# Gain of queries and keys moved into the rope tables, low halves one window later, attention steps in a new order

## The chip, the cores and the metric

The kernel runs on one NeuronCore of one Trainium2 chip. The metric is the device time of one execution in microseconds (us). The engines are called as the profile calls them: PE is TensorE, DVE is VectorE, ACT is ScalarE, POOL is GpSimd, SP is SyncE, which here only issues DMAs. Each engine works through its own list in order; only semaphores tie the lists together.

## What is computed

Two transformer blocks, 256 tokens wide 1024. The first has adaLN modulation, a retention group and a differential attention group that share one input projection, an output projection and a product-key expert layer; the second a feed-forward, a gated mixer with a state-space part, another feed-forward and a gate. The change touches the attention of the first block alone, and what runs beside it:

```
def diff_softmax_attend(q, k, v, lam):
    s = jnp.einsum('bhpqd,bhpkd->bhpqk', q, k).astype(jnp.float32) * (DIFF_D ** -0.5)
    p = jax.nn.softmax(s, axis=-1)
    a = (p[:, :, 0] - lam * p[:, :, 1]).astype(v.dtype)
    return jnp.einsum('bhqk,bhke->bhqe', a, v)
...
    q = apply_rope(qk_heads(dq, qk_norm_g[0]), cos, sin)
    k = apply_rope(qk_heads(dk, qk_norm_g[1]), cos, sin)
    kc = qk_heads(cdk, qk_norm_g[1])
```

`qk_heads` cuts a row of 512 into 8 pieces of 64, divides each by its root mean square and multiplies it by a gain `g` of 64 numbers, one for queries and one for keys. `apply_rope` is `x * cos + rot(x) * sin`, where `rot` swaps neighbouring groups of 16 and changes a sign. The keys of the context (`kc`) get the gain but no rope. There are 4 heads with 2 maps each, 256 queries (2 blocks of 128) and 512 keys (256 of the context, 256 of the sequence).

## The kernel before

Weights stream from DRAM in 257 chunks of 1 MB through three buffers (`raw`). A chunk is two halves, and most halves `u` are split in two: ACT copies the high part (`w_hi`), DVE subtracts it to get the low part (`w_lo`). PE multiplies high by high, high by low and low by high, all accumulated in PSUM, so it needs both parts. There are four slots of each. SP issues a chunk when the low parts of the chunk three earlier are made.

The first stage, about the first 227 us of 1717, is the one that is changed. Its work is one list, written by hand in `front_steps`. Each engine's program walks through the same list and does its own part of each step, so the place of a step in the list sets its order on PE, DVE and ACT at once. The steps that matter:

- `win(p, h)` is a **window**: PE does one half of the input projection, pass p (0 to 5, groups of 512 columns in the order 3, 4, 5, 0, 1, 2), quarter h (0 to 3). Passes 0, 1, 2 and 4 have four token tiles and full width, pass 3 has its two context tiles at half width, pass 5 has two tiles only. On ACT and DVE a window means `ahead`: they make high and low parts up to three windows in front of PE.
- `evac p`: ACT copies the finished pass from PSUM (4 or 2 instructions).
- `mod n`: one column block of the adaLN modulation, one DVE instruction over 128x1024 and a short read of its accumulator.
- `square n`, `unit n`, `rope n`: normalisation and rope of queries (n = 0, 1), keys (2, 3) and context keys (4, 5, no rope); rope 4, 5 are the retention group's. In `unit`, DVE sums the squares, multiplies the 512 columns by the gain, waits for ACT's square root and inverts it; for keys it also multiplies by the result.
- `qturn h`, `kturn h`: PE transposes (2 or 4 of 128x128), ACT copies the result. `kturn 0` waits for `s_qk` 6, which is the end of unit 5.
- `score n` (n = 0 to 7: block n // 4, head n % 4): PE two score matmuls of 512 columns; DVE the `combine` of n - 1 (1 / sum, factor, `aa = E1 * c + E0`, L1992), then two maxima (L2199); ACT two exponentials. `turn n`: PE transposes `aa` (L1069), ACT copies it to `aT`. `weigh n`: PE `aT` by the values. After `weigh 3` and `weigh 7` ACT also scales and squares four heads.
- `rturn`, `mask`, `madd`, `rscore`, `rweigh`, `dnorm`, `dblocks`: the retention group's transposes, decay masks, scores and sums, and the turned attention result. `out n` is the output projection; PE's first `out` ends the stage.

Score n + 1, weigh n - 1 and turn n stand together between windows, with the window in front of them as cover for the combination. At three places no window stands there: score 2, weigh 0, turn 1; score 4, weigh 2, turn 3; weigh 6, turn 7, rturn 0. Lines of helpers: L911 is every matmul, L992 the transposes of `head_turn`, L1069 those of `turn`, L1511 every ACT instruction, L1980 DVE's tensor_tensor, L2000 its sums, L2004 its reciprocals, L2136 `mod`. `ar` is the arena that holds nearly all intermediate tiles, `cols` and `rows` are small tables, `pb` is PSUM.

Of the kernel before, what the change touches and what calls it, by code (L numbers as in the profile page):

```python
# [12 lines left out]
ACT = mybir.ActivationFunctionType  # L13
# [149 lines left out]
def front_steps():  # L163


    steps = []

    def mods(*ns):
        steps.extend(("mod", n) for n in ns)

    def win(p, h, *more):
        steps.append(("win", p, h))
        steps.extend(more)

# [12 lines left out]
    steps.extend([("whalf", 3), ("cturn", 2), ("crows", 2)])  # L187
    win(0, 3, ("evac", 0))
# [8 lines left out]
    win(2, 0, ("square", 2), ("square", 3), ("unit", 2), ("qturn", 0), ("qturn", 1))  # L197
    mods(22)
    win(2, 1, ("rope", 2), ("unit", 3), ("qturn", 2), ("qturn", 3))
    mods(23)  # L200
    win(2, 2, ("rope", 3), ("square", 4), ("square", 5))
    mods(24)
    win(2, 3, ("evac", 2), ("unit", 4))
    win(3, 0, ("unit", 5))
    mods(25, 26)
    win(3, 1, ("kturn", 0), ("kturn", 1))
    mods(27)
    win(3, 2, ("kturn", 2), ("kturn", 3), ("score", 0))
    mods(28)
    win(3, 3, ("evac", 3), ("score", 1), ("turn", 0))  # L210
    mods(29)
    steps.extend([("score", 2), ("weigh", 0), ("turn", 1)])
    win(4, 0, ("score", 3), ("weigh", 1), ("turn", 2))
    mods(30, 31)
    steps.extend([("score", 4), ("weigh", 2), ("turn", 3)])
    win(4, 1, ("score", 5), ("weigh", 3), ("turn", 4), ("rope", 4))
    mods(32, 33)
    win(4, 2, ("score", 6), ("weigh", 4), ("turn", 5), ("rope", 5))
    mods(34, 35)
    win(4, 3, ("evac", 4), ("score", 7), ("weigh", 5), ("turn", 6))  # L220
    mods(36, 37)
    mods(38, 39)
    steps.extend([("weigh", 6), ("turn", 7), ("rturn", 0)])
    win(5, 0, ("mask", 0), ("weigh", 7))
    win(5, 1, ("rturn", 1), ("mask", 1), ("madd", 0))
    win(5, 2, ("rscore", 0), ("mask", 2), ("dvar", 0), ("madd", 1))
    win(5, 3, ("added", 1), ("droot", 0), ("rscore", 1), ("evac", 5), ("madd", 2), ("dnorm", 0))
# [170 lines left out]
def program(nc, wall, keys_d, cols_d, rows_d, bigrows_d, crow_d, wmod_d, dist_d, x_d, ctx_d, pT_d, gws_d, out_d, n_chunks):  # L398
    assert n_chunks * 2 == U_END
    with ExitStack() as es:  # L400
# [380 lines left out]
        def heads8(ap):  # L781
            return ap.rearrange("p (h d) -> p h d", d=64)
# [124 lines left out]
        def tensor_program(e):  # L907
# [109 lines left out]
            for name, n, *more in FRONT:  # L1017
# [24 lines left out]
                elif name == "kturn":  # L1042
                    t.wait_ge(s_qk, 6)
                    if n >= 2:
                        t.wait_ge(s_heads, 4 + n - 1)
                    head_turn(5 + n % 2 * 2, [pj(i, 2048 + n * 128, 2176 + n * 128) for i in range(4)])
                elif name == "rturn":
# [8 lines left out]
                elif name == "score":  # L1056
                    i, h = n // 4, n % 4
                    for p in range(2):
                        t.wait_ge(s_heads, 8)
                        if n:  # L1060
# [440 lines left out]
        def scalar_program(e):  # L1501
            a = Engine(e, s_a)
            made = 0
# [122 lines left out]
            for name, n, *more in FRONT:  # L1626
# [346 lines left out]
        def vector_program(e):  # L1973
# [31 lines left out]

            def ahead(u, only=False):
# [145 lines left out]
            def unit(n, ap):  # L2152
# [4 lines left out]
                ts(r_, r_, 1.0 / 64, EPS, MUL, ADD, sig=s_qn)  # L2157
                g_ = qkg[:, 0:64] if n < 2 else qkg[:, 64:128]
                tt(heads8(ap), heads8(ap), bc(g_, 1, 8), MUL)
                v.wait_ge(s_qs, n + 1)  # L2160
# [48 lines left out]
            for name, n, *more in FRONT:  # L2209
# [32 lines left out]
                elif name == "win" and (n, *more) != (5, 3):  # L2242
                    ahead(HALF_OF[(name, n, *more)])
                elif name == "unit":
                    v.wait_ge(s_wev, group_done(3 if n < 2 else 4))
                    unit(n, pj(n, 1536, 2048) if n < 2 else pj(n - 2, 2048, 2560))
                elif name == "rope":
                    if n < 2:
                        rope(pj(n, 1536, 2048), n, s_qk)
                    elif n < 4:  # L2250
                        rope(pj(n - 2, 2048, 2560), n - 2, s_qk)
                    else:
                        v.wait_ge(s_wev, group_done(0))
                        rope(pj(n - 4, 0, 512), n - 4, s_rk)
                elif name == "added":
# [635 lines left out]
```

## Time and profile before

| | |
|---|---|
| median of 3 runs | 1717.91 us (1717.3 to 1718.87) |
| profiled execution, its own time | 1718.86 us |
| its span in the trace | 1717.1 us |
| PE / DVE / ACT busy, share of the span | 96% / 74% / 56% |
| HBM | 184 GB/s over the span |
| first stage, to PE's first `out` matmul | 226.45 us |

The profiled execution is 0.95 us above the median, which is inside the spread of the runs, so differences read from the trace may be taken off the median as they stand. Times in the rows below count from the start of the span.

### The profile page before, as it was taken

To read this page: it belongs to the slowest core of one execution; us is meant where nothing else is said; L and a number is where in the kernel's file an instruction comes from. 1 tells how busy PE (TensorE), PEld (TensorE's weight loads), DVE (VectorE), ACT (ScalarE), POOL (GpSimd) and SP (SyncE) were. 2 spreads that over 40 slices of the span, in tenths; PEclk is the share of its full clock that TensorE was granted. 3 is DMA by queue.
4 is the path that set the end of the run, shared out by engine and by line. 5 is a ranking of instruction groups with operands and counts; after the bars stand their busy time and mean duration, and the time that the engine had idled before them with its cause. 6 is when DMAs were issued, how large, how long until landed. Compare 5 with 4: busy or idle time off the path is not lost.

```text
span 1717.1 us, 26934 instructions
## 1 busy us (share of the span) xinstructions
PE 1640.3 (96%) x10312; PEld 1398.2 (81%) x10312; DVE 1276.1 (74%) x2066; ACT 968.9 (56%) x1343; POOL 73.3 (4%) x46
## 2 busy tenths in 40 slices
PE   8988788998999999999999999999998989999997
PEld 3776578998999888888888888788888778788886
DVE  2686666899888899987777766776666787676666
ACT  4555455554455554555555555665556767665556
POOL 0000003532000000000000000000000000000000
PEclk9999898999999999999999999999999999999999
DMA  8643334445655555566656565455544533554552
GB/s 319 248 177 120 100 131 148 148 164 193 195 187 188 179 194 213 191 220 252 219 208 214 193 226 185 166 193 199 191 177 160 196 135 135 184 215 172 196 192 78
DMA packets 53267, 317.86 MB, mean 185 GB/s; under 512 B 5937, under 2 KB 6097, under 8 KB 19218
## 3 DMA queue, kind: packets, MB, share of 16 engines
q1 hardware_dynamic: 51954, 310.08, 51.0%
q0 software_dynamic: 1184, 6.05, 0.9%
q8 instruction: 82, 1.34, 0.3%
q14 instruction: 47, 0.39, 0.1%
HBM read 306.64 MB, written 9.47 MB: 184 GB/s over the span
## 4 chain that ended last, share of the span: by engine, by line
PE 75%; DVE 17%; ACT 5%; issue 1%; DMA 1%; DVEq 0%; ACTq 0%; SPq 0%
PE pb L911 74%; DVE w_lo L1980 4%; DVE ar L1980 4%; ACT ar L1511 2%; DVE ar L1992 2%; ACT w_hi L1511 1%; DVE ar L2136 1%; DVE ar L2342 1%; DVE ar L2339 1%; DMA raw<-in_wall 1%; ACT L1511 1%; DVE ar L2346 1%; DVE sm L2199 0%; DVE ar L1985 0%; ACT HX L1511 0%
## 5 line engine op out<-in xcount | busy, mean ns | idle before, releaser
L1980 DVE TENSOR_TENSOR w_lo<-raw,w_hi 128x1024 fp32r<-128x1024 f32 x471 | 577.3, 1226 | 198.1 <-ACT w_hi L1511 166.6
L1511 ACT ACTIVATE w_hi<-raw 128x1024 fp32r<-128x1024 f32 x498 | 528.7, 1062 | 144.2 <-PE pb L911 103.2
L911 PE MATMUL pb<-HX,w_hi 128*128 128x256 f32 (+1 forms) x2752 | 509.0, 332 | 7.6 <-DVE HX L1980 3.5
L911 PEld LDWEIGHTS pb<-HX,w_hi 128*128 128x128 f32 x2752 | 413.8, 192 | 51.0 <-issue 4.0
L911 PE MATMUL pb<-w_hi,HC 128*128 128x512 f32 (+1 forms) x1648 | 443.9, 391 | 4.4 <-DVE HC L1992 3.3
L911 PEld LDWEIGHTS pb<-w_hi,HC 128*128 128x128 f32 x1648 | 302.3, 188 | 65.2 <-issue 3.8
L1511 ACT ACTIVATE ar<-pb 128x256 f32<-128x256 f32 (+2 forms) x320 | 153.4, 480 | 327.1 <-PE pb L911 221.1
L1980 DVE TENSOR_TENSOR ar<-ar 128x512 bf16<-128x512 bf16 (+7 forms) x494 | 263.3, 568 | 44.9 <-ACT ar L1511 21.3
L911 PE MATMUL pb<-HX,w_lo 128*128 128x256 f32 x1952 | 279.3, 284 | 2.5 <-DVE w_lo L1980 2.2
L911 PEld LDWEIGHTS pb<-HX,w_lo 128*128 128x128 f32 x1952 | 263.9, 192 | 14.5 <-DVE w_lo L1980 3.3
L911 PE MATMUL pb<-w_lo,HC 128*128 128x512 f32 (+1 forms) x824 | 252.9, 388 | 0.0
L911 PEld LDWEIGHTS pb<-w_lo,HC 128*128 128x128 f32 x824 | 154.6, 188 | 32.5
L911 PE MATMUL pb<-w_hi,HX 128*128 128x512 f32 x512 | 145.0, 406 | 3.5 <-ACT w_hi L1511 2.0
L911 PE MATMUL pb<-ar 128*128 128x64 bf16 (+3 forms) x1960 | 125.6, 222 | 19.3 <-ACT ar L1511 9.2
L911 PEld LDWEIGHTS pb<-ar 128*128 128x128 bf16 (+2 forms) x1960 | 104.6, 119 | 42.2 <-issue 19.8
L911 PEld LDWEIGHTS pb<-w_hi,HX 128*128 128x128 f32 x512 | 95.9, 194 | 25.3 <-ACT w_hi L1511 4.3
L1511 ACT ACTIVATE ar<-ar 128x512 f32<-128x512 f32 (+8 forms) x112 | 66.9, 597 | 75.8 <-DVE ar L1980 31.5
L1511 ACT ACTIVATE HC<-ar 128x512 fp32r<-128x512 f32 (+1 forms) x89 | 55.4, 623 | 83.0 <-PE pb L911 46.9
L1980 DVE TENSOR_TENSOR ar<-pb,ar 128x512 f32<-128x512 f32 (+1 forms) x86 | 58.4, 680 | 52.2 <-ACT ar L1511 44.2
L1980 DVE TENSOR_TENSOR HC<-ar,HC 128x512 fp32r<-128x512 f32 (+1 forms) x89 | 60.6, 681 | 32.4 <-ACT HC L1511 27.7
L911 PE MATMUL pb<-w_lo,HX 128*128 128x512 f32 x256 | 81.4, 400 | 0.5 <-DVE w_lo L1980 0.3
L2738 POOL TENSOR_TENSOR w_lo<-raw,w_hi 128x1024 fp32r<-128x1024 f32 x27 | 64.9, 2404 | 104.3 <-ACT w_hi L1511 63.6
(146 smaller groups left out, 688.9 us busy)
## 6 DMA issues: line engine op xcount, KB each, us to landing
raw<-in_wall SPq DMA_DIRECT2D x257, 1024.0 KB, 4.8
ar<-in_wmod SPq DMA_DIRECT2D x24, 512.0 KB, 3.8
act_keep<-ar SPq DMA_DIRECT2D x28, 256.0 KB, 5.6
ar<-act_keep SPq DMA_DIRECT2D x28, 256.0 KB, 5.0
x<-in_wmod SPq DMA_DIRECT2D x8, 512.0 KB, 5.2
ar<-in_bigrows POOLq DMA_DIRECT2D x2, 1024.0 KB, 5.0
ar<-acs_keep POOLq DMA_DIRECT2D x2, 1024.0 KB, 8.8
x<-in_x SPq DMA_DIRECT2D x1, 1024.0 KB, 9.6
```

The lines of the kernel that those rows point to most:

```text
L911: return e.matmul(o, l, r, start=start, stop=stop, skip_group_check=True)
L1511: a.did(e.activation(out, in_, func, scale=scale, **kw), sig)
L1980: v.did(e.tensor_tensor(out, a_, b_, op), sig)
L1992: v.did(e.scalar_tensor_tensor(out, a_, s_, b_, op0, op1), sig)
L2136: v.did(e.scalar_tensor_tensor(w, w, 1.0, c_, MUL, MUL, accum_out=modT[:, n, 0:1]), s_modv)
L2339: v.did(e.max(vals[:, c_], src))
L2342: v.did(e.max_index(idx[:, c_], vals[:, c_], src))
L2346: v.did(e.match_replace(src, vals[:, c_], src, NEG))
L2738: p.did(e.tensor_tensor(w_lo[:, made % NH, :], raw_half(w), w_hi[:, made % NH, :].bitcast(F32), SUB), s_lop)
```

## The change

- **Gain.** `unit` no longer multiplies by the gain. A new step `ropetab`, once, multiplies the cosine and sine tables by the gains of queries and keys (six small DVE instructions, into unused columns of `yv`). Rope 0 to 3 use these tables. The context keys, which have no rope, get the gain when ACT copies the turned keys: that copy of 512 columns becomes two of 256, the second with a scale per partition (`kg`, one new column of `cols`). The tensors behind `cols` keep their addresses.
- **Rope** writes its swapped half in two DVE instructions of 256 columns, where there were four of 128.
- **Low parts.** On DVE `ahead` reaches two windows in front of PE from pass 1 on (three before). The high parts stay three in front.
- **Banks and waits.** `kturn` uses PSUM banks 7 and 6 (5 and 7 before), so it doesn't share a bank with the scores, and a score waits for its own head's keys alone; `turn` waits for all.
- **Order.** `qturn` stands in front of the squares and units of its window. Squares 4, 5 and units 4, 5 stand behind window (2, 3), evac 2. The key turns stand one window earlier, the scores, turns and weighings are spread so that a window stands in front of each, up to (5, 2). `mod` steps move to fit, and with them the places of their DMAs, which are worked out from the list.

```
-                tt(heads8(ap), heads8(ap), bc(g_, 1, 8), MUL)
...
+            def rope_tables():
+                v.wait_ge(s_tab, 32)
+                for z in range(2):
+                    g_ = qkg[:, 64 * z:64 * z + 64]
+                    tt(scaled_cos[z].rearrange("p (t d) -> p t d", t=2), col("cos").rearrange("p (t d) -> p t d", t=2),
+                       bc(g_, 1, 2), MUL, free=True)
...
+                    for b in range(2):
+                        tt(so[:, :, :, b, :], si[:, :, :, b, :], bc(ga[:, :, 1 - b, :], 1, 2), MUL, free=True)
...
-                    for a_ in range(2):
-                        tt(tv[:, :, a_, b, :], xv[:, :, a_, 1 - b, :], bc(sv[:, a_, b, :], 1, 8), MUL, free=True)
+                    tt(tv[:, :, :, b, :], xv[:, :, :, 1 - b, :], bc(sv[:, :, b, :], 1, 8), MUL, free=True)
...
-                while made < (ORD[u] + 1 if only else REACH[u]):
+                while made < (ORD[u] + 1 if only else REACH[u] - late):
...
-                    ahead(HALF_OF[(name, n, *more)])
+                    ahead(HALF_OF[(name, n, *more)], late=int(n >= 1))
...
-                    act(kTd[:, n, :], PB[5 + n % 2 * 2][:, :], ACT.Copy, sig=s_heads)
+                    act(kTd[:, n, 0:256], PB[7 - n % 2][:, 0:256], ACT.Copy)
+                    act(kTd[:, n, 256:512], PB[7 - n % 2][:, 256:512], ACT.Copy, scale=col("kg"), sig=s_heads, free=True)
...
-                        t.wait_ge(s_heads, 8)
+                        t.wait_ge(s_heads, 4 + h + 1)
...
-    win(2, 3, ("evac", 2), ("unit", 4))
-    win(3, 0, ("unit", 5))
+    win(2, 3, ("evac", 2), ("square", 4), ("square", 5), ("unit", 4), ("unit", 5))
```

**DVE, from window (0, 3) to rope 0.** Before; the two `w_lo` are those of windows (0, 3) and (1, 0), the instruction on `ar<-ar,rows` is the gain, L2136 is mod 18:

```order
30 L1980 TENSOR_TENSOR w_lo<-raw,w_hi 128x1024
31 L2136 SCALAR_TENSOR_TENSOR ar,modT<-ar 128x1024
32 L1980 TENSOR_TENSOR w_lo<-raw,w_hi 128x1024
33 L1980 TENSOR_TENSOR HC<-fsc,HC 128x256 x2
34 L2000 TENSOR_REDUCE ar<-ar 128x8
35 L1987 TENSOR_SCALAR ar<-ar 128x8
36 L1980 TENSOR_TENSOR ar<-ar,rows 128x512
37 L2004 RECIPROCAL ar<-ar 128x8
```

Now, on the same engine and the same stretch (lines are three further on):

```order
30 L1983 TENSOR_TENSOR w_lo<-raw,w_hi 128x1024
31 L1983 TENSOR_TENSOR ar<-cols,rows 128x128
32 L1983 TENSOR_TENSOR ar<-cols,rows 128x4x16 x2
33 L1983 TENSOR_TENSOR ar<-cols,rows 128x128
34 L1983 TENSOR_TENSOR ar<-cols,rows 128x4x16 x2
35 L2139 SCALAR_TENSOR_TENSOR ar,modT<-ar 128x1024
36 L1983 TENSOR_TENSOR HC<-fsc,HC 128x256 x2
37 L2003 TENSOR_REDUCE ar<-ar 128x8
38 L1990 TENSOR_SCALAR ar<-ar 128x8
39 L2007 RECIPROCAL ar<-ar 128x8
```

The low part of window (1, 0) has moved behind the first unit, the six table instructions stand in its place, and the reciprocal follows the short scalar step directly.

**PE, from window (4, 3) to window (5, 1).** Before; 128x512 on `ar` are score matmuls, 128x128 on `ar` are weighings, L1069 are turns, L992 is rturn:

```order
181 L911 MATMUL pb<-w_hi,HC 128x512 x4
182 L911 MATMUL pb<-w_lo,HC 128x512 x2
183 L911 MATMUL pb<-ar 128x512 x2
184 L911 MATMUL pb<-ar 128x128 x4
185 L1069 MATMUL pb<-cols,ar 128x128 x4
186 L911 MATMUL pb<-ar 128x128 x4
187 L1069 MATMUL pb<-cols,ar 128x128 x4
188 L992 MATMUL pb<-cols,ar 128x128 x6
189 L911 MATMUL pb<-w_hi,HX 128x512 x4
190 L911 MATMUL pb<-w_lo,HX 128x512 x2
```

Now, from the second tile of window (5, 0) on; score 6, weigh 4 and turn 5 stand three rows before it:

```order
185 L912 MATMUL pb<-w_hi,HX 128x512 x4
186 L912 MATMUL pb<-w_lo,HX 128x512 x2
187 L912 MATMUL pb<-ar 128x512 x2
188 L912 MATMUL pb<-ar 128x128 x4
189 L1071 MATMUL pb<-cols,ar 128x128 x4
190 L912 MATMUL pb<-w_hi,HX 128x512 x4
191 L912 MATMUL pb<-w_lo,HX 128x512 x2
192 L912 MATMUL pb<-w_hi,HX 128x512 x4
193 L912 MATMUL pb<-w_lo,HX 128x512 x2
194 L912 MATMUL pb<-ar 128x128 x4
195 L1071 MATMUL pb<-cols,ar 128x128 x4
196 L993 MATMUL pb<-cols,ar 128x128 x6
```

Before, score 7, weigh 5, turn 6, weigh 6, turn 7 and rturn 0 stood in one piece. Now window (5, 0) ends before score 7, weigh 5, turn 6, and window (5, 1), two tiles, stands before weigh 6, turn 7, rturn 0.

## Rows read from the trace of the kernel before

**Rows 1.** The page, part 1: busy us (share of the span) xinstructions.
```profile
PE 1640.3 (96%) x10312; PEld 1398.2 (81%) x10312; DVE 1276.1 (74%) x2066; ACT 968.9 (56%) x1343; POOL 73.3 (4%) x46
```

**Rows 2.** Windows: stretch, length, busy of each engine, PEclk, DMA share, GB/s.
```profile
60.00:93.00 33.00, 33.00 (x153) 27.26 (x152) 24.82 (x60) 19.55 (x31) 0.00 (x0) 1.00 0.51 185
93.00:120.60 27.60, 23.22 (x113) 18.76 (x111) 25.26 (x46) 14.43 (x23) 0.00 (x0) 1.00 0.41 152
120.60:211.70 91.10, 76.81 (x356) 57.47 (x356) 58.01 (x108) 46.78 (x96) 0.00 (x0) 0.91 0.35 122
```

**Rows 3.** Waits in 93:227 us, one each of PE, DVE: us, times, longest.
```profile
PE pb L1069 <- DVE ar L1992: 6.9, 3, 3.3
...
DVE w_lo L1980 <- ACT w_hi L1511: 22.4, 7, 5.7
```

**Rows 4.** Timeline of DVE: start, duration, line, instruction [idle before <-releaser].
```profile
69.20 0.43 DVE L1980 TENSOR_TENSOR HC<-fsc,HC 128x256 fp32r<-128x256 f32 x1 [1.82 <-ACT HC L1511]
...
96.76 0.69 DVE L1980 TENSOR_TENSOR ar<-ar,rows 128x512 f32<-128x512 f32 x1
97.56 0.20 DVE L2004 RECIPROCAL ar<-ar 128x8 f32<-128x8 f32 x1
...
98.59 1.23 DVE L2136 SCALAR_TENSOR_TENSOR ar<-ar 128x1024 f32<-128x1024 f32 x1
...
99.93 1.23 DVE L1980 TENSOR_TENSOR w_lo<-raw,w_hi 128x1024 fp32r<-128x1024 f32 x1
101.19 1.50 DVE L1980 TENSOR_TENSOR ar<-ar,cols 128x512 f32<-128x512 f32 x5
102.72 0.69 DVE L1980 TENSOR_TENSOR ar<-ar 128x512 f32<-128x512 f32 x1
```

**Rows 5.** Timeline of ACT: square root of unit 2, one exponential of score 5.
```profile
96.76 0.21 ACT L1511 ACTIVATE ar<-ar 128x8 f32<-128x8 f32 x1 [0.53 <-DVE ar L1987]
...
166.61 0.78 ACT L1511 ACTIVATE ar<-pb,sm,ar 128x512 f32<-128x512 f32 x1 [4.11 <-DVE sm L1980]
```

**Rows 6.** Timeline of PE: key turns, a whole iteration, and the stage's last steps.
```profile
120.66 1.55 PE L992 MATMUL pb<-cols,ar 128*128 128x128 f32 x8 [1.99 <-DVE ar L1980]
121.87 2.05 PE L911 MATMUL pb<-w_hi,HX 128*128 128x512 f32 x4
...
157.64 1.18 PE L911 MATMUL pb<-w_hi,HX 128*128 128x512 f32 x4
...
163.29 2.22 PE L911 MATMUL pb<-ar 64*128 64x512 f32 x12
165.34 0.60 PE L1069 MATMUL pb<-cols,ar 128*128 128x128 f32 x4
165.70 1.17 PE L911 MATMUL pb<-w_hi,HX 128*128 128x512 f32 x4
...
206.75 1.99 PE L911 MATMUL pb<-ar 64*128 64x256 f32 x8 [1.05 <-ACT ar L1511]
...
211.07 0.61 PE L911 MATMUL pb<-w_lo,HX 128*128 128x512 f32 x2
...
226.45 1.61 PE L911 MATMUL pb<-w_hi,HC 128*128 128x512 f32 x4 [2.49 <-DVE HC L1992]
```

**Rows 7.** Timeline of DVE: combination 4, maxima 5, and the stage's end.
```profile
163.86 0.16 DVE L2004 RECIPROCAL sm<-ar 128x1 f32<-128x1 f32 x1
...
165.05 1.28 DVE L2199 TENSOR_REDUCE sm<-pb 128x1 f32<-128x512 f32 x2
166.37 0.16 DVE L1980 TENSOR_TENSOR sm<-sm,ar 128x2 f32<-128x2 f32 x1
...
212.58 1.50 DVE L1992 SCALAR_TENSOR_TENSOR ar<-pb,ar 128x512 f32<-128x512 f32 x2
...
225.48 1.65 DVE L1992 SCALAR_TENSOR_TENSOR HC<-pb,cols,HC 128x256 fp32r<-128x256 f32 x4
```

**Rows 8.** The page, part 6, weight chunks: count, KB each, us to landing.
```profile
raw<-in_wall SPq DMA_DIRECT2D x257, 1024.0 KB, 4.8
```

More of the change, by code:

```diff
@@ L196, in front_steps @@
     mods(21)
-    win(2, 0, ("square", 2), ("square", 3), ("unit", 2), ("qturn", 0), ("qturn", 1))
+    win(2, 0, ("qturn", 0), ("qturn", 1), ("square", 2), ("square", 3), ("unit", 2))
     mods(22)
-    win(2, 1, ("rope", 2), ("unit", 3), ("qturn", 2), ("qturn", 3))
+    win(2, 1, ("qturn", 2), ("qturn", 3), ("rope", 2), ("unit", 3))
     mods(23)
-    win(2, 2, ("rope", 3), ("square", 4), ("square", 5))
+    win(2, 2, ("rope", 3))
+    win(2, 3, ("evac", 2), ("square", 4), ("square", 5), ("unit", 4), ("unit", 5))
@@ L202, in front_steps @@
     mods(24)
-    win(2, 3, ("evac", 2), ("unit", 4))
-    win(3, 0, ("unit", 5))
[L205 to L212, printed above, removed]
-    win(4, 0, ("score", 3), ("weigh", 1), ("turn", 2))
-    mods(30, 31)
-    steps.extend([("score", 4), ("weigh", 2), ("turn", 3)])
-    win(4, 1, ("score", 5), ("weigh", 3), ("turn", 4), ("rope", 4))
@@ L217, in front_steps @@
-    mods(32, 33)
-    win(4, 2, ("score", 6), ("weigh", 4), ("turn", 5), ("rope", 5))
+    win(3, 0, ("kturn", 0), ("kturn", 1))
+    mods(25)
+    win(3, 1, ("kturn", 2), ("kturn", 3), ("score", 0))
+    mods(26)
+    win(3, 2, ("score", 1), ("turn", 0))
+    mods(27, 28)
+    win(3, 3, ("evac", 3), ("score", 2), ("weigh", 0), ("turn", 1))
+    mods(29, 30)
+    win(4, 0, ("score", 3), ("weigh", 1), ("turn", 2))
+    mods(31, 32)
+    win(4, 1, ("score", 4), ("weigh", 2), ("turn", 3), ("rope", 4))
@@ L219, in front_steps @@
+    mods(33)
+    win(4, 2, ("score", 5), ("weigh", 3), ("turn", 4), ("rope", 5))
     mods(34, 35)
-    win(4, 3, ("evac", 4), ("score", 7), ("weigh", 5), ("turn", 6))
+    win(4, 3, ("evac", 4), ("score", 6), ("weigh", 4), ("turn", 5))
     mods(36, 37)
[L222 to L226, printed above, removed]
@@ L227, in front_steps @@
-    win(5, 3, ("added", 1), ("droot", 0), ("rscore", 1), ("evac", 5), ("madd", 2), ("dnorm", 0))
+    win(5, 0, ("score", 7), ("weigh", 5), ("turn", 6))
+    mods(38)
+    win(5, 1, ("weigh", 6), ("turn", 7), ("rturn", 0), ("mask", 0))
+    mods(39)
+    win(5, 2, ("weigh", 7), ("rturn", 1), ("mask", 1), ("madd", 0))
+    win(5, 3, ("rscore", 0), ("mask", 2), ("dvar", 0), ("madd", 1), ("added", 1), ("droot", 0), ("rscore", 1), ("evac", 5),
+        ("madd", 2), ("dnorm", 0))
     steps.extend([("rweigh", 0), ("rscore", 2), ("mask", 3), ("rweigh", 1), ("dblocks", 0), ("madd", 3)])
@@ L616, in program @@
         s1, s2 = yv[:, 0, 0:512], yv[:, 1, 0:512]
+        scaled_cos = [yv[:, 0, 512 + 256 * z:640 + 256 * z] for z in range(2)]
+        scaled_sin = [yv[:, 0, 640 + 256 * z:768 + 256 * z] for z in range(2)]
         mrow = [yv[0:2, b, 512:1024] for b in range(2)]
@@ L1043, in tensor_program @@
                     t.wait_ge(s_qk, 6)
-                    if n >= 2:
+                    if n:
                         t.wait_ge(s_heads, 4 + n - 1)
-                    head_turn(5 + n % 2 * 2, [pj(i, 2048 + n * 128, 2176 + n * 128) for i in range(4)])
+                    head_turn(7 - n % 2, [pj(i, 2048 + n * 128, 2176 + n * 128) for i in range(4)])
                 elif name == "rturn":
@@ L2004, in rcp, with ahead @@
                 v.did(e.reciprocal(out, a_), sig)
-            def ahead(u, only=False):
+            def ahead(u, only=False, late=0):
                 nonlocal made
-                while made < (ORD[u] + 1 if only else REACH[u]):
+                while made < (ORD[u] + 1 if only else REACH[u] - late):
                     w = SPLIT[made]
@@ L2246, in vector_program @@
                     unit(n, pj(n, 1536, 2048) if n < 2 else pj(n - 2, 2048, 2560))
+                elif name == "ropetab":
+                    rope_tables()
                 elif name == "rope":
                     if n < 2:
-                        rope(pj(n, 1536, 2048), n, s_qk)
+                        rope(pj(n, 1536, 2048), n, s_qk, scaled_cos[0], scaled_sin[0])
                     elif n < 4:
-                        rope(pj(n - 2, 2048, 2560), n - 2, s_qk)
+                        rope(pj(n - 2, 2048, 2560), n - 2, s_qk, scaled_cos[1], scaled_sin[1])
                     else:
                         v.wait_ge(s_wev, group_done(0))
-                        rope(pj(n - 4, 0, 512), n - 4, s_rk)
+                        rope(pj(n - 4, 0, 512), n - 4, s_rk, col("cos"), col("sin"))
                 elif name == "added":
```

16 lines of the change are left out of this document (9 added, 7 removed).

## The prediction, made before the changed kernel was run

> **What bounds the kernel now.** I read the busy shares first. PE is busy 96% of the span and DVE 74% [rows 1], so a saving on DVE counts only where PE stands still for it. The table of windows says where that is: PE is busy all of 60 to 93 us, then 23.2 of 27.6 us, then 76.8 of 91.1 us [rows 2]. In the second of these stretches DVE is busy 25.3 of 27.6 us and bounds; in the third no engine is near full, and the granted clock of PE is 0.91. A mean of 0.91 is a mix of its two levels, 2.4 GHz and 1.2 GHz, with 18% of the time (16.4 us) at the lower one. The waits name two links: turns of `aa` wait 6.9 us for the combinations, and DVE waits 22.4 us for high parts that ACT makes in the same step [rows 3]. The timeline then gives the three dates on which I hang the sum: key turn 0 at 120.66, end of window (5, 3) at 211.7, first `out` at 226.45 [rows 6]. Behind `out` nothing is changed, so what `out` gains the end gains, as long as weights arrive.
>
> **Part 1, to key turn 0 (DVE bounds).** Removed in front of it: six gain products, 0.80 us each from start to next start [rows 4]. But the reciprocal behind each now meets ACT's square root, which it did not before: the root starts with the product at 96.76 and takes 0.21 [rows 5], so with two handoffs about 0.3 of each 0.8 comes back; 6 x 0.5 = 3.0 us. Rope: the first five instructions take 101.19 to 102.72 [rows 4]; one of 512 columns needs about 0.73, so the four of 128 take 0.20 each. The trace has no such instruction of 256 columns. It lies between 0.20 (no cost for length) and 0.40 (no fixed cost); on the line through the sizes shown it is 0.35 to 0.38. Then two of them cost 0.7 to 0.75 where four cost 0.8: 0.1 for each of four ropes, 0.4 us, with bounds 0 and 1.6. One low part fewer (99.93 to 101.19, 1.3) and one mod fewer (98.59 to 99.93, 1.3) stand in front of unit 5. The softplus exchange with ACT in `gammas` doesn't follow fully, since ACT comes to it out of a PSUM copy bound by PE: 0.3 us back. The tables are six instructions, four of them at 0.20 and two of about 0.3, 1.4 us with bounds 1.2 and 2.2. They stand where DVE idled 1.82 us before the context's low parts [rows 4], and the low part of window (1, 0), 1.3 us, has left the same place, so 3.1 us cover them: nothing. If that cover were gone they would cost 1.4. Sum: 3.0 + 0.4 + 1.3 + 1.3 - 0.3 = 5.7, key turn 0 at 115.0. PE gets there earlier still: it came at 118.7 (120.66 less 1.99), window (3, 1), 4.2 us as worked out below, now stands behind the turn, and of the 4.4 us that PE idled in stretch two [rows 2] the 2.4 that were not this wait were for the query turns' copy, which now stands in front of the squares, and for a PSUM copy. So PE comes at 112.1 and waits 2.9 us instead of 1.99. I expect the clock to fall as it fell after that 1.99: the next four matmuls took 2.05 against 1.18 at full clock [rows 6]. For turns and window together 1.8 us.
>
> **Part 2, to the end of window (5, 3).** PE's own work: 76.8 busy, less half of the 16.4 us at the lower clock, is 68.6 us at full clock [rows 2]. Window (3, 1) comes in: a full window takes 157.64 to 163.29, 5.65 for four tiles, so two full and two half tiles 4.2. Retention score 0 leaves, 2.0 [rows 6]. So 70.8 us, and with the clock's 1.8 PE alone could end at 115.0 + 72.6 = 187.6. Do the chains keep up? PE's iteration is 157.64 to 165.70, 8.06 us: window 5.65, score and weighing 2.05, turn 0.36 [rows 6]. From the end of a score: maxima 1.5, exponentials 2 x 0.9 [rows 5, 7], combination 1.2 (163.86 to 165.05), 4.5 us in all, and a turn comes 1.0 + 0.4 + 5.65 + 2.05 = 9.1 after that score. DVE also does two mods (2.7) and a low part (1.3): 6.7 us, with a rope 8.9. The low part's high part was made one window ago, so the DVE-on-ACT waits of rows 3 go. I walked the list with these numbers: score 0 at 122.9 (129.4 before), turn 0 at 129.4 after 0.3 of waiting for the combination, turn 1 at 136.1, turn 2 at 144.1, turn 3 at 152.2, turn 4 at 160.3, turn 5 at 168.3, each without a wait. In pass 5 a window has two tiles, 2.85 us, and no longer covers DVE's 6.7: turn 6 waits 1.2 and comes at 174.7, weigh 6 waits 0.8 for ACT's copy, turn 7 0.4 and comes at 180.0. Windows (5, 2) and (5, 3), weigh 7 and rturn 1 end at 188.3 (before 211.7). The split copies of turned keys, 0.2 us more on ACT each, lie beside windows: nothing. Low parts are there 7 us before PE wants them, except at (3, 0), where DVE is done at 107.1 and PE asks at 108.4.
>
> **Part 3, to `out`.** Retention score 0 waits for ACT's copy of rturn 1, to 188.8. Before, DVE's products of score 0 started at 212.58 and the low parts that release `out` at 225.48 [rows 7], 12.9 us. Now mask 2 is in that chain as before, the products start 1.0 after their score, the second has to wait 0.3 for its half, and one low part more (the one put off) stands in it, 1.3: 12.9 + 1.3 + 0.3 = 14.5, then 1.0 to `out`. 188.8 + 1.0 + 14.5 + 1.0 = 205.3, a gain of 21.2 us. The walk leaves out handoffs on some ten links, 0.06 to 0.1 us each, 0.8 us. **Gain 20.4 us**.
>
> **Queues.** SP issues a chunk when low parts are made, so one window (5.65 us) later. A chunk lands in 4.8 us [rows 8] and its high part is made some four windows after the issue: covered, and 5 us at worst if not. Mod DMAs move with the list; mod 36, the tightest, is issued when mod 32 is done, about 147, and used about 170. POOL's only part here is the gate row after weigh 7; it follows.
>
> **Rivals.** (a) **The clock stays low**: gaps of 2.9 us at the key turn and 0.4 to 1.2 us around pass 5 leave PE at 1.2 GHz over pass 5 too. Each stretch costs about 2 us, as the key turn's; two to four of them, 4 to 7 us: gain 13 to 17. For it: 18% of stretch three was at the low level. Against: PE's waits there shrink from 14.3 us to about 3. The Trainium skill (TensorE: Matmul & The Clock Gate, HAM oscillation) says that short runs of matmuls between waits bring the clock down every time; the drops of rows 2 agree, and by it they should go with the gaps. (b) **Only the DVE savings count**: the chain score, exponential, combination is longer than I take it, for each window ends on it as turns did before. Then key turn 0's 5.7 us stays, and of the turns' 6.9 us of waiting [rows 3] some part up to the whole: gain 6 to 12, time 1706 to 1712. (c) **Nothing moves**: PE is 96% busy, and what the stage gives is taken back behind it, where weights or the expert layer set the pace: 1717.9. The Trainium skill (Perfetto Trace Analysis, Identifying the Most-Contended Engine) says to work on the engine with the highest occupancy first; by that DVE edits give 0. Rows 2 speak against it, with 18.7 us of PE idle in two stretches, and that page's Optimization Strategy allows for a bottleneck that changes with the regime. (d) **Slower: low parts come last.** With the reach cut to two, if DVE is over one window behind PE from (3, 0) on, PE waits in each of the 12 windows to (5, 3) for one mod and one low part, 2.6 us: 31 us, against 20 gained, 1728. It decides once DVE's slack falls from 7 us under 0. Against: DVE's 6.7 to 8.9 us a window against 8.06.
>
> **How the numbers follow.** Forecast case, gain 18 to 24: 0.70. (a) 0.14, (b) 0.09, (c) 0.03, (d) 0.04. The profiled execution's sum goes off the median as it stands: 1717.9 - 20.4 = 1697.5. The forecast case reaches 1694 to 1700; the bounds of rope and tables add 1.2 below and 2 above; with (a) to 1705 that holds 0.84. Range 1693 to 1705.5. A measurement tells about 0.2% (3.4 us) from no change. Faster 0.93, same 0.03, slower 0.04.
>
> **What would show it.** Right: no DVE wait on `w_hi` between 120 and 190; key turn 0 at 115 with 2.9 us of PE idle before it; turns 1 to 5 some 8.1 us apart without waits; first `out` at 206. Wrong: turns 1 to 5 each after a wait (b), granted clock under 0.9 in 170 to 190 (a), PE waiting for `w_lo` (d), or `out` at 206 and an end that is not 20 us earlier (c).

## The result, and the profile after

The changed kernel takes 1699.1 us (median of 4 runs, 1697.9 to 1702.5), against 1718.2 for the kernel before on the same chip: a ratio of 0.9892, with a 95% interval of 0.9875 to 0.9910, or 19.1 us. Run again word for word on two later occasions it took 1699.2 both times. The prediction was 1697.5, in a range of 1693 to 1705.5. The profiled execution has a span of 1697.4 us and took 1699.2.

The busy shares of the page (compare [rows 1]) hardly differ: DVE lost 4.4 us of 1276, PE 8.5 of 1640.

```profile
PE 1631.8 (96%) x10312; PEld 1394.2 (82%) x10312; DVE 1271.7 (75%) x2054; ACT 969.6 (57%) x1347; POOL 72.7 (4%) x46
```

Its span is 19.7 us shorter (1717.1 to 1697.4). 11.2 of that is idle time of PE that is gone; the other 8.5 is PE's busy time, for the same 10312 matmuls, and it goes with the higher granted clock of the stretch that follows the key turns. The table of windows (columns as in [rows 2]), cut at key turn 0, at retention score 0 and behind the first `out`:

```profile
60.00:93.00 33.00, 33.00 (x153) 27.30 (x152) 24.17 (x61) 20.56 (x32) 0.00 (x0) 1.00 0.45 157
93.00:115.00 22.00, 18.41 (x90) 15.56 (x89) 18.88 (x35) 11.53 (x20) 0.00 (x0) 0.94 0.45 167
115.00:190.00 75.00, 71.85 (x368) 54.83 (x367) 59.93 (x104) 46.60 (x99) 0.00 (x0) 0.97 0.45 155
190.00:208.00 18.00, 12.64 (x70) 9.99 (x69) 14.31 (x25) 13.55 (x21) 1.22 (x2) 0.90 0.25 84
208.00:1697.00 1489.00, 1445.95 (x9456) 1264.90 (x9454) 1133.23 (x1788) 848.73 (x1136) 71.16 (x39) 0.99 0.52 185
```

From 115 to 190 PE is busy 71.85 of 75 us, at a granted clock of 0.97; before, the like stretch had 76.8 of 91.1 at 0.91 [rows 2]. The last line answers to the rest of the program: 1489 us before too, with 1445.6 us of PE.

All waits of PE in 93 to 210 us (total, times, longest), which answer to [rows 3]; none is for a low part or for weights:

```profile
PE pb L993 <- DVE ar L1983: 3.6, 1, 3.6
PE pb L912 <- DVE HC L1995: 2.7, 1, 2.7
PE pb L927 <- DVE ar L1983: 1.9, 1, 1.9
PE pb L912 <- ACT ar L1513: 1.5, 2, 1.0
PE pb L1071 <- DVE ar L1995: 1.5, 2, 1.2
PE pb L912 <- DVE ar L1995: 0.8, 1, 0.8
```

And this is all that DVE waited for between 120 and 190 us; the wait on `w_hi`, 22.4 us in 93 to 227 us before, is not among it:

```profile
DVE sm L2212 <- PE pb L912: 6.3, 4, 4.5
```

The timeline of DVE (compare [rows 4]): the tables, the idle time behind them, a unit without its gain product, the one unit (2) that waits longer for its square root, and a rope:

```profile
63.27 1.03 DVE L1983 TENSOR_TENSOR ar<-cols,rows 128x128 f32<-128x128 f32 x6
...
67.85 0.43 DVE L1983 TENSOR_TENSOR HC<-fsc,HC 128x256 fp32r<-128x256 f32 x1 [2.22 <-ACT HC L1513]
...
109.93 0.17 DVE L1990 TENSOR_SCALAR ar<-ar 128x8 f32<-128x8 f32 x1
110.38 0.20 DVE L2007 RECIPROCAL ar<-ar 128x8 f32<-128x8 f32 x1 [0.28 <-ACT ar L1513]
...
95.06 0.20 DVE L2007 RECIPROCAL ar<-ar 128x8 f32<-128x8 f32 x1 [0.71 <-ACT ar L1513]
...
72.82 2.09 DVE L1983 TENSOR_TENSOR ar<-ar 128x512 f32<-128x512 f32 x4
```

The same rope, read from a view that is cut at 74 us and so ends with its third instruction:

```profile
72.82 1.36 DVE L1983 TENSOR_TENSOR ar<-ar 128x512 f32<-128x512 f32 x3
```

The timeline of PE (compare [rows 6]): key turn 0 and what follows it, key turns 2 and 3, some turns of `aa`, retention score 0, the first `out`:

```profile
113.56 1.97 PE L993 MATMUL pb<-cols,ar 128*128 128x128 f32 x8 [3.58 <-DVE ar L1983]
115.18 2.05 PE L912 MATMUL pb<-w_hi,HX 128*128 128x512 f32 x4
...
121.23 1.03 PE L993 MATMUL pb<-cols,ar 128*128 128x128 f32 x8
...
143.77 0.60 PE L1071 MATMUL pb<-cols,ar 128*128 128x128 f32 x4
151.83 0.60 PE L1071 MATMUL pb<-cols,ar 128*128 128x128 f32 x4
159.89 0.60 PE L1071 MATMUL pb<-cols,ar 128*128 128x128 f32 x4
...
174.87 0.66 PE L1071 MATMUL pb<-cols,ar 128*128 128x128 f32 x4 [1.18 <-DVE ar L1995]
...
180.31 0.66 PE L1071 MATMUL pb<-cols,ar 128*128 128x128 f32 x4 [0.33 <-DVE ar L1995]
...
189.68 5.88 PE L912 MATMUL pb<-ar 64*128 64x256 f32 x32 [0.98 <-ACT ar L1513]
...
206.10 2.05 PE L912 MATMUL pb<-w_hi,HC 128*128 128x512 f32 x4 [2.67 <-DVE HC L1995]
```

Turns 2, 3 and 4 are 8.06 us apart and wait for nothing. The granted clock was 0.50 over key turn 0 (113.56 to 115.50 us) and 1.00 in 170 to 190 us, where the last turns stand:

```profile
113.56:115.50 1.94, 1.94 (x9) 1.94 (x10) 1.78 (x3) 0.82 (x3) 0.00 (x0) 0.50 0.00 0
170.00:190.00 20.00, 16.96 (x92) 13.07 (x91) 15.09 (x26) 14.63 (x34) 0.00 (x0) 1.00 0.22 83
```

The stage's end on DVE, with the products of retention score 0, the last two low parts, and the low parts that release `out` (compare [rows 7]):

```profile
190.84 0.69 DVE L1995 SCALAR_TENSOR_TENSOR ar<-pb,ar 128x512 f32<-128x512 f32 x1 [4.12 <-PE pb L912]
...
197.18 2.55 DVE L1983 TENSOR_TENSOR w_lo<-raw,w_hi 128x1024 fp32r<-128x1024 f32 x2
...
205.13 1.65 DVE L1995 SCALAR_TENSOR_TENSOR HC<-pb,cols,HC 128x256 fp32r<-128x256 f32 x4
```

**A common origin.** The start of a program, before anything that the change touches, differs by up to 2.1 us between executions. Its last common step is DVE's low part of window (0, 3): at 63.48 us before, at 62.13 after, and between 62.03 and 64.14 in all profiles. So dates of different kernels are compared below as the time since that step. From it to the first `out` ("the stage") before took 162.97 us and the changed kernel 143.97: 19.0 us, all but 0.1 of the gain. From `out` to the end it is 1490.7 and 1491.3.

### The profile page after: what moved, and what is told of

It reads as the page before. It is cut to its first block, busy times and chain, and to the rows that moved or that the text cites. A ratio compares the mean times of both kernels' runs of the same rounds, so it can differ in the third digit from the quotient of the medians.

```text
span 1697.4 us, 26926 instructions
## 1 busy us (share of the span) xinstructions
PE 1631.8 (96%) x10312; PEld 1394.2 (82%) x10312; DVE 1271.7 (75%) x2054; ACT 969.6 (57%) x1347; POOL 72.7 (4%) x46
## 4 chain that ended last, share of the span: by engine, by line
PE 77%; DVE 16%; ACT 4%; DMA 1%; issue 1%; DVEq 0%; SPq 0%; ACTq 0%
PE pb L912 76%; DVE w_lo L1983 4%; DVE ar L1983 4%; DVE ar L1995 2%; ACT ar L1513 2%; DMA raw<-in_wall 1%; ACT w_hi L1513 1%; DVE ar L2357 1%; DVE ar L2354 1%; ACT L1513 1%; DVE ar L2139 1%; DVE ar L2361 1%; DVE ar L1999 0%; DVE sm L2212 0%; ACT HX L1513 0%
## 5 line engine op out<-in xcount | busy, mean ns | idle before, releaser
L1983 DVE TENSOR_TENSOR ar<-ar 128x512 bf16<-128x512 bf16 (+9 forms) x506 | 268.5, 566 | 44.6 <-ACT ar L1513 21.0
L912 PEld LDWEIGHTS pb<-HX,w_lo 128*128 128x128 f32 x1952 | 264.4, 192 | 14.5 <-DVE w_lo L1983 3.3
```

The lines of the kernel that those rows point to most:

```text
L912: return e.matmul(o, l, r, start=start, stop=stop, skip_group_check=True)
L1983: v.did(e.tensor_tensor(out, a_, b_, op), sig)
```

## The experiments

Three names for the parts of the change: the fold (gain in the tables, ropes of two parts), the late low parts, and the order. Theory: the three parts take away three different waits of one chain between DVE and PE, so each has its own price and they nearly add: the fold and the order bring key turn 0, the late low parts take DVE's waiting for ACT out of the turns. Rivals: only the DVE work saved counts, or late low parts are a risk and no gain. All experiments are copies of one of the two kernels with the edit that is shown.

### The fold alone

The kernel before, in its order and with its early low parts, gets the tables, the units without gain products, ropes of two parts and the split copy of turned keys.

```diff
-                g_ = qkg[:, 0:64] if n < 2 else qkg[:, 64:128]
-                tt(heads8(ap), heads8(ap), bc(g_, 1, 8), MUL)
...
-                    for a_ in range(2):
-                        tt(tv[:, :, a_, b, :], xv[:, :, a_, 1 - b, :], bc(sv[:, a_, b, :], 1, 8), MUL, free=True)
+                    tt(tv[:, :, :, b, :], xv[:, :, :, 1 - b, :], bc(sv[:, :, b, :], 1, 8), MUL, free=True)
```

> The order, banks and reach of before, with the gain folded into the rope tables and rope in two instructions. Theory (PE gains what it stood still for): key turn 0 comes when PE arrives, at most 2.0 us earlier plus the 1.8 us of low clock behind that wait, and about 1 us at the query turns: 1718.2 - 4 = 1714, between 1713 and 1716. Rival (the DVE work itself is what counts, 3.4 us before the key turn and 0.2 after): the same 3.5 us, but then key turn 0 would still wait. Rival (most-occupied engine alone counts): 1718.

Measured: 1714.5 us, ratio 0.9977 (0.9967 to 0.9987), 3.7 us off. PE, at key turn 0:

```profile
117.16 1.09 PE L994 MATMUL pb<-cols,ar 128*128 128x128 f32 x8 [0.25 <-DVE ar L1983]
```

It came 53.74 us after the common step, against 57.18 before: 3.44 us, for which the prediction had 3.0 + 0.4. The wait of 1.99 us is 0.25, and PE is at full clock. DVE is still the last to come: the turn moved by all that DVE saved, and PE came 1.7 us earlier too. The turns of `aa` wait as before (6.8 us against 6.9), so this part has nothing to do with them.

### The late low parts alone

```diff
-                while made < (ORD[u] + 1 if only else REACH[u]):
+                while made < (ORD[u] + 1 if only else REACH[u] - late):
...
-                    ahead(HALF_OF[(name, n, *more)])
+                    ahead(HALF_OF[(name, n, *more)], late=int(n >= 1))
```

> Before, with DVE's low parts two windows ahead of PE in place of three, nothing else. Theory: the 22 us that DVE waits for high parts of the same step go; combinations of scores 0 to 7 come up to 1.3 us plus that wait earlier, key turn 0 1.3 us earlier, and one low part more stands before out: a gain of 3 to 7 us, 1711 to 1715. Rival (d), low parts come last: PE waits for low parts from window (3, 0) on and the kernel is slower than 1718. Rival (reach is only a cover, and the turns wait for the exponentials): within 1 us of 1718.

Measured: 1711.7 us, ratio 0.9958 (0.9941 to 0.9974), 6.5 us off. The waits of DVE and PE in 93 to 227 us:

```profile
DVE w_lo L1980 <- ACT w_hi L1511: 5.0, 3, 3.4
...
PE pb L1069 <- DVE ar L1992: 3.1, 3, 2.1
```

22.4 us of DVE waiting for ACT became 5.0, and 6.9 us of PE waiting for combinations became 3.1 [rows 3]. Key turn 0 did not move (57.14 against 57.18): the one low part fewer ahead of it stood where DVE idles anyway, and that idle time only grew (from 1.82 to 3.13 us). Rival (d), in which low parts come last, is refuted: no wait of PE for `w_lo` shows in 93 to 227 us here, nor in the changed kernel. Part of the stage's 6.0 us is the clock's, though: this execution kept the full clock at key turn 0 after 1.94 us of waiting, where the profile before had not after 1.99, and from key turn 0 to key turn 2 it took 5.12 us against 6.73. That is 1.6 us which the edit did not buy.

### The changed kernel with one part undone

Early low parts in the changed kernel:

```diff
-                    ahead(HALF_OF[(name, n, *more)], late=int(n >= 1))
+                    ahead(HALF_OF[(name, n, *more)], late=0)
```

> The changed kernel with the reach of before (low parts three windows ahead). Theory: low parts wait for high parts again (over 10 us of DVE waits on w_hi between key turn 0 and window (5, 3)), the combinations behind them come later, turns 0 and 6 wait about 2 us each, key turn 0 is 1.3 us later; against that one low part leaves the end of the stage: 1699 + 1 to 4, 1700 to 1703. Rival (the order alone is the gain): 1699 or under.

Measured: 1706.8 us, ratio 0.9938 (0.9922 to 0.9955): 7.7 us lost against the changed kernel, more than I had expected. DVE waits 13.0 us for `w_hi` again, and five turns wait, 8.1 us in all. The stage took 147.49 us, 3.5 more than 143.97; but this execution kept the full clock at key turn 0, after the same idle time, and the turn came 51.41 us after the common step, not 1.3 later as I had expected:

```profile
114.83 1.09 PE L993 MATMUL pb<-cols,ar 128*128 128x128 f32 x8 [3.59 <-DVE ar L1983]
```

The gain products and ropes of four parts in the changed kernel (the first edit above undone, with the tables and the split copy left out again):

> The changed kernel with gain products in the units and four-part ropes of before, no tables. Theory: key turn 0 is 3.4 us later (six times 0.5 and four times 0.1) and nothing behind it catches up, as PE bounds from there: 1699.1 + 3.4 = 1702.5, and PE's wait before the key turn grows from 3.6 to about 7. Rival (PE's gap only shifts and the clock is low anyway): under 1701.

Measured: 1705.7 us, ratio 0.9927 (0.9910 to 0.9943), 6.6 us lost, again more than expected.

```profile
116.89 1.97 PE L993 MATMUL pb<-cols,ar 128*128 128x128 f32 x8 [5.93 <-DVE ar L1982]
```

Key turn 0 came 54.86 us after the common step against 51.43: 3.43 us, which shows as 5.93 us of waiting in place of 3.58. That it is the price of the old order (3.44) is chance: DVE idles 0.48 us ahead of the last reciprocal here, once, for a reason that the profile doesn't show. Without that the fold is worth some 3.0 us in the new order, as the kernel with the order alone, below, confirms (54.47 against 51.41 for order and fold). The stage is 3.8 us longer. So of the 6.6 us, 2.8 are not in this stage of this execution; 2.0 of them lie behind the first `out` (1493.3 us to the end, against 1491.3).

### The order alone

The changed kernel with both of these undone: its order of steps, PSUM banks and turns are what is left of the change.

> The changed kernel's order, PSUM banks and turns, with the gain products and the four-part ropes of before and the low parts where they stood before: neither the fold nor the late low parts. From the low part of window (0,3) to the first out before takes 163.0 us and the changed kernel 144.0; the fold alone took 4.1 off and the late low parts alone 6.0. If the parts add, this kernel takes 163.0 - (19.0 - 4.1 - 6.0) = 154.1 us there, and its time is about 1709 us. If the parts overlap (each alone relieves the same VectorE chain, and the order makes its own use of it), it is nearer to the two runs with one part undone: 144.0 + 3.5 + 3.8 = 151.3 us, 1706 us.

Measured: 1709.8 us, ratio 0.9941 (0.9927 to 0.9954), 9.5 us off; the stage took 153.2 us. As they stand, both are nearer the additive case (154.1, 1709) than the overlapping one (151.3, 1706). The stages don't decide it, though: they hold the clock's drops at key turn 0, of which this execution and the changed kernel's had one and the two singles none. With the drops taken out, as in the last table below, the additive case is 148.1, the overlapping one 151.2, and this kernel 150.4. Key turn 0 came 2.71 us earlier than before, at 54.47: one mod and one low part fewer in front of it, 2.6 us in the prediction. PE's waits in 93 to 227 us, and below them one of the kernel before:

```profile
PE pb L1071 <- DVE ar L1994: 8.0, 5, 2.5
PE pb L993 <- DVE ar L1982: 5.7, 1, 5.7
...
PE pb L912 <- ACT ar L1513: 1.6, 2, 1.0
```

```profile
PE pb L911 <- ACT ar L1511: 8.1, 6, 2.7
```

The order by itself makes PE come to key turn 0 far too early, and its turns of `aa` wait no less than before (8.0 against 6.9). What it takes away is another wait, which neither the prediction's list of links nor the theory above names: matmuls of PE (scores, weighings, retention scores) that wait for ACT, 8.1 us before, 7.4 with the fold alone, 7.7 with the late low parts alone, 1.6 here and 1.5 in the changed kernel. Turn 7 comes 0.8 us earlier than before (128.75 against 129.58), and by then PE has also done windows (5, 0) and (5, 1), which stood behind it; from there to `out` it is 24.5 us against 33.4. Which single move of the order brings how much of the 9.5 us was not tried.

### The price of the clock

In the changed kernel 28 useless transposes (3.2 us) go into the gap ahead of key turn 0:

```diff
                 elif name == "kturn":
+                    if n == 0:
+                        t.wait_ge(s_qk, 4)
+                        for j in range(28):
+                            e.transpose(PB[7][:, (j % 2) * 128:(j % 2) * 128 + 128], pj(j % 2, 2048, 2176), ident)
                     t.wait_ge(s_qk, 6)
```

> The changed kernel, with 28 useless transposes (about 3.4 us) in TensorE's queue in the 3.6 us gap ahead of key turn 0; they go to the bank that the turn overwrites, and need rows that were ready long before. Nothing else is changed, so the turn still waits for VectorE's last key rope. It tells the price of the wait from the price of the low clock behind it. My theory: the turn comes when it came (51.4 us after the last low part of window (0, 3)), but at the full clock: 1.09 us instead of 1.97, the window behind it 4.2 us instead of about 6.6, and all that follows 1 to 2.5 us earlier (the two profiles of the changed kernel have turns 2 and 3 at 59.1 and 58.1 us after that low part): 56.5 us there, and the time 1696.5 to 1698.5 against 1699.2. Rival: VectorE's chain to score 0 and the combinations bounds what follows, so an earlier window changes nothing: first out at 142.9 to 144.0 us and 1699.

Beside it, and once before, the changed kernel word for word:

> The changed kernel itself, word for word, beside e9_key_gap_filled on the same chip: 1697 to 1701 us, key turn 0 after 3.6 us of idle time at the low clock (1.97 us) as in the two profiles so far.

> The changed kernel itself, word for word, on the chip of the others: 1697 to 1702 us. It shows whether the key turn at the head of the last window falls to the low clock again after its wait (1.97 us for eight transposes in the first profile; an otherwise similar wait of 3.6 us left it at the full clock in another kernel), and how far the times of one kernel spread.

PE in the three, the filled one first, each with the turn and (in the two copies) the matmuls behind it:

```profile
111.80 3.22 PE L1047 MATMUL pb<-cols,ar 128*128 128x128 f32 x28
115.54 1.09 PE L993 MATMUL pb<-cols,ar 128*128 128x128 f32 x8 [0.53 <-DVE ar L1987]
```

```profile
114.90 1.97 PE L993 MATMUL pb<-cols,ar 128*128 128x128 f32 x8 [3.59 <-DVE ar L1983]
116.52 1.77 PE L912 MATMUL pb<-w_hi,HX 128*128 128x512 f32 x4
```

```profile
115.02 1.97 PE L993 MATMUL pb<-cols,ar 128*128 128x128 f32 x8 [3.58 <-DVE ar L1983]
116.64 1.90 PE L912 MATMUL pb<-w_hi,HX 128*128 128x512 f32 x4
```

Filled, the turn came when it always came (51.40 us after the common step), and all behind it came earlier. From key turn 0 to key turns 2 and 3 the filled kernel took 5.10 us, the copies 6.50 and 6.64, the first profile of the changed kernel 7.67. These 1.4 to 2.6 us are all that the low clock cost there, and they reach the first `out`: the stage took 141.49 us filled, 142.84 and 142.93 in the copies, 143.97 in the first profile. Less what the clock cost, the three are at 141.4 to 141.5 too. The times, 1698.3 us filled and 1699.2 beside it, differ by 1.0 with intervals that overlap (ratios 0.9863 to 0.9896 and 0.9871 to 0.9904): the trace shows it, the medians agree and don't prove it. The rival, that DVE bounds what follows, falls by the stage, in this one trace.

### A better place for two mods, and for two low parts

```diff
-    mods(22)
...
-    mods(23)
...
-    mods(24)
+    mods(22, 23)
     win(3, 0, ("kturn", 0), ("kturn", 1))
-    mods(25)
+    mods(24, 25)
```

> The changed kernel, with VectorE's modulation of blocks 22 and 23 (two steps of 1.3 us) put behind the key unit of the last self half instead of ahead of it. My theory: the key turn at the head of the last window waits for VectorE's chain (3.6 us idle in the changed kernel), so it comes 2.7 us earlier and TensorE's idle time there falls to about 0.9 us; scores, turns and the first out follow 2 to 3 us earlier, since VectorE has idle time between there and score 0. Time 1694 to 1697 us (changed kernel: 1699.1). Rival: the modulation that now stands later delays VectorE's next low parts or the query unit, the wait moves to a later turn, and the time stays 1698 to 1700.

Measured: 1696.9 us, ratio 0.9872 (0.9857 to 0.9886), against 1699.2 (0.9873 to 0.9902) for the changed kernel beside it: 2.3 us, with intervals that just overlap.

```profile
111.70 1.09 PE L991 MATMUL pb<-cols,ar 128*128 128x128 f32 x8 [1.54 <-DVE ar L1981]
...
125.08 0.66 PE L1069 MATMUL pb<-cols,ar 128*128 128x128 f32 x4 [0.74 <-DVE ar L1993]
...
202.43 2.04 PE L910 MATMUL pb<-w_hi,HC 128*128 128x512 f32 x4 [2.78 <-DVE HC L1993]
```

Key turn 0 came at 49.39, 2.0 us earlier where 2.7 were expected (DVE now idles 0.73 us for ACT ahead of unit 4), and at full clock. Both theories were partly right: turn 0 now waits 0.74 us for DVE, which has the moved mods in front of it, and so comes 1.4 us earlier than in the filled kernel and not 2.0. The stage took 140.12 us, 2.8 less than the changed kernel's beside it; 1.5 of that is the clock's drop that did not come.

Then, on top of it, the last two low parts behind `dblocks`, where DVE has nothing urgent:

```diff
-                    if n == 1:
-                        ahead(HALF_OF["win", 5, 3])
                 elif name == "dvar":
...
                 elif name == "dblocks":
                     turn(TB_DIFF, 4)
+                    ahead(HALF_OF["win", 5, 3])
```

> The kernel of e5_mods_behind_keys, and VectorE's last two low parts (2.55 us, between score 1 and dblocks) put behind dblocks. My theory: the tail from score 0 to the first out is bound by VectorE's chain, so out comes another 1.5 to 2.6 us earlier: 1692 to 1695 us. Rival: ScalarE's chain (evacuations and the gate's turn) ends at the same point and out comes at most 0.5 us earlier, or the low parts are then awaited by the products behind out: the same time as e5.

Measured: 1693.7 us, ratio 0.9850 (0.9835 to 0.9864), 5.5 us better than the changed kernel beside it, with intervals that are apart. PE and DVE around `out`:

```profile
202.68 1.16 PE L910 MATMUL pb<-w_hi,HC 128*128 128x512 f32 x4 [1.18 <-DVE HC L1993]
...
203.81 2.56 DVE L1981 TENSOR_TENSOR w_lo<-raw,w_hi 128x1024 fp32r<-128x1024 f32 x2
```

`out` came 138.80 us after the common step, 1.3 earlier (1.5 to 2.6 expected), with half the wait, and at full clock: four such matmuls take 1.16 us against 2.04. Retention score 3, which stands behind the first `out`, came at 141.72 against 145.51, 3.8 us earlier; the two medians differ by 3.2. So the low clock behind the 2.78 us wait had cost 2.5 us, more than the 1.3 by which `out` came earlier. This is the best of the versions run.

## Why the prediction was right, and where it was off

Dates since the common step. The prediction's are its own less 63.48, without the 0.8 us that it set aside for handoffs at the end, and are called the walk below, since it walked the list of steps; "filled" is the kernel without the clock's drop at key turn 0.

| | key turn 0 | turn 0 | turn 4 | turn 5 | turn 6 | turn 7 | score 0 | `out` |
|---|---|---|---|---|---|---|---|---|
| predicted | 51.5 | 65.9 | 96.8 | 104.8 | 111.2 | 116.5 | 125.3 | 141.8 |
| changed, first profile | 51.43 | 66.74 | 97.76 | 105.93 | 112.74 | 118.18 | 127.55 | 143.97 |
| changed, beside the filled | 51.42 | 65.57 | 96.63 | 104.80 | 111.61 | 117.05 | 126.42 | 142.84 |
| filled | 51.40 | 64.14 | 95.19 | 103.37 | 110.17 | 115.62 | 124.99 | 141.49 |

- **Part 1, 5.7 us: measured 5.75.** The order gave 2.71 (one mod and one low part, 2.6) and the fold on top of it 3.04 (3.0 + 0.4 - 0.3 = 3.1). The late low part gives nothing here: 57.14 against 57.18. The reciprocal does meet the root, with 0.28 us of waiting in five of six units. From the short scalar step to the reciprocal it is 1.00 us before and 0.44 now, so a gain product was worth 0.56 and not 0.80 (I had 0.5). In unit 2 the reciprocal waits 0.71: in the new order ACT's copy of the query turn, 0.86 us, stands ahead of that root. The prediction did not have this, and it is the 0.4 us by which the two singles (3.44 + 2.71 = 6.15) exceed the whole. The softplus exchange took back 0.45 (DVE waits 0.73 there, 0.28 before), where the prediction had 0.3; the ropes gave 0.13 each and not 0.1. That the sum is right to 0.1 is in part luck: what unit 2 lost, the other products had more than I gave them. A part of 256 columns costs some 0.33 us, where I had 0.35 to 0.38: one instruction of 512 and two of 256 take 1.36, and one of 512 alone 0.69. The tables cost nothing, as said: 1.03 us (I had 1.4), and DVE still idled 2.22 us behind them.
- **PE's wait at key turn 0, 2.9 us: measured 3.6.** PE came 0.8 us earlier than I had it. That wait is DVE's date less PE's, so it changed nothing but the odds on the clock.
- **The clock, 1.8 us: measured 2.6, 1.5 and 1.4.** This term differs from execution to execution. In the profile beside the filled kernel, in which it was 1.4, turns 0 to 5 stand within 0.4 us of the walk; in the first, in which it was 2.6, all are 0.8 to 1.1 late. Rival (a) took the clock for low over pass 5; its sign was a clock under 0.9 in 170 to 190, and it was 1.00 there. Where it did fall is a place that no term has: behind the 2.67 us wait at the first `out`, whose four matmuls take 2.05 us where they took 1.61 before. From there to retention score 3 it is 5.28 us against 4.51, and 2.92 at full clock.
- **Part 2: turns 1 to 5 without waits, as walked, 8.06 us apart (8.17 from turn 4 to 5).** The prediction counted only PE's waits for the combinations; the fall of its waits for ACT, from 8.1 us to 1.5, is in its result all the same, since it took PE's own work as the bound. Turn 6 waits 1.18 (1.2), weigh 6 0.56 (0.8), turn 7 0.33 (0.4). What is off is small: 0.4 us more on the way from turn 5 to turn 6, and 0.98 us instead of 0.5 for ACT's copy of the last turn ahead of score 0. Together 0.9 us, about the 0.8 that I had set aside for handoffs. In the first profile `out` is 2.2 us later than the walk: those 0.8, 0.8 of the clock, and 0.6 that is left.
- **Part 3, 16.5 us from score 0 to `out`: measured 16.42.** DVE's chain was 14.3 (14.5).
- **Behind `out` nothing changed, rival (c):** 1490.7 us before, 1491.3 after, 1487.5 to 1493.3 in all profiles. So `out`, 20.35 us earlier from the span's start, is 19.0 earlier by the common step, and the rest is an earlier start of that execution. That it stands at 206.10, to a tenth where the sum had it (205.3 + 0.8), is luck: 1.35 us of early start cover what the stage fell short. The gain was 1.3 us too high, 20.4 against 19.1. The prediction worked out from the Trainium skill (Perfetto Trace Analysis, Identifying the Most-Contended Engine) that DVE edits give 0. They did not: PE is at 96%, and DVE edits alone gave 3.7 and 6.5 us, since the 4% that PE idles stand in part where DVE's chain is last. The Trainium skill goes on (Perfetto Trace Analysis, Optimization Strategy) to look for the gaps on that engine and for what blocks it there; that agrees with these runs.
- **Rival (b)** falls: turns waited 6.9 us before and 1.5 after. Neither the order alone (8.0) nor order and fold (8.1) brings that; the late low parts do.

How the parts add, as stages since the common step, the clock's cost at key turn 0 taken out of each (its time from key turn 0 to 2, less 5.1; only there, so it is rough for the kernels of the old order):

| | stage | less the clock | median less before, same chip |
|---|---|---|---|
| before | 162.97 | 161.3 | 0 |
| fold alone | 158.88 | 158.9 | -3.7 |
| late low parts alone | 157.01 | 157.0 | -6.5 |
| order alone | 153.20 | 150.4 | -9.5 |
| order and fold | 147.49 | 147.5 | -11.4 |
| order and late low parts | 147.79 | 145.1 | -12.5 |
| all | 143.97 | 141.4 | -19.1 |

By the singles' medians the sum is 19.7, and 19.1 came. By the stages less the clock the singles give 2.4, 4.3 and 10.9, together 17.6, where 19.9 came. On top of the order the fold is worth 2.9 and the late low parts 5.4, and together 9.0. That the parts nearly add is shown to within some 2 us, and not closer. What stays open: by medians the last part to be put on gains more than its stage (7.7 against 6.1, 6.6 against 3.7). The surplus is 1.6 and 2.9 us. Of the second, 2.0 lie behind the stage in the profiled execution; of the first nothing does in the profiled execution, which took 3.8 us less from `out` to the end than the changed kernel's, so it is in other executions. The kernel with early low parts spread over 9 us (1700.2 to 1709.3), and its profile is of its fastest run, so this profile can't say where the rest of its median went.

## What to carry to other kernels

Look for where the busiest engine idles, and price an edit of another engine only there: 96% busy left room for 19 us, and each edit was worth its instructions on the chain that ended last, less the partner that it then met (0.24 of every 0.80 us). Make an operand late enough that its producer on the other engine has long been done: here DVE spent 22.4 us waiting for high parts that ACT made in the same step, and moving the low parts alone took 6.5 us off. Put independent work between a producer and PE's use of it: the order alone brought PE's waits for ACT from 8.1 to 1.6 us. Once an edit shortens one side of a meeting, move what does not belong in front of it (two mods, two low parts: 5.5 us more), and count the slow clock behind a gap as part of the gap's price.

## What the runs showed of the hardware

The same idle time did not always bring the clock down at key turn 0. After 3.58, 3.58 and 3.59 us of idle PE the eight transposes took 1.97 us (granted clock 0.50, which is 1.2 GHz), after 3.59 us in a fourth profile 1.09 (1.00, 2.4 GHz); after 1.99 us 1.55, after 1.94 us 1.09; after 5.74 and 5.93 us 1.97 both times, after 1.53 and 1.54 us 1.09 both times. At the first `out` shorter waits did it: after 2.34 to 2.78 us of idle PE four matmuls took 2.04 or 2.05 us in seven profiles; after 2.67 us in the kernel with late low parts alone, whose PE had not waited in the 8 us before, they took 1.17. In the changed kernel PE had waited 1.93 us one step earlier. And once down it came back at different times: the stretch to key turn 2 took 7.67, 6.64, 6.50 us in three executions of one kernel, 5.10 at full clock. The Trainium skill (TensorE: Matmul & The Clock Gate, HAM oscillation) tells of a re-throttle after each wait between short bursts; of the four waits of 3.58 and 3.59 us three agree, with a price of 1.4 to 2.6 us each, and the fourth does not. In a sum such a gap is better entered as a chance than as a fixed term. A gap filled with useless transposes kept the clock, in a single trial.

Executions of one kernel on one core spread: 1696.3 to 1702.5 us in 13 runs of the changed kernel, 1700.2 to 1709.3 in four of the one with early low parts.
